# A mixture-of-experts layer on one core: slot tables in two transfers and one expert ahead, and the spare rows' turn and second product in other places

## The reference

```python
for l in range(DEPTH):                      # DEPTH = 1, SEQ = D_MODEL = 1024
    proj = x @ w_in[l]
...
    mix = jnp.concatenate([y_conv, y_sb, y_gla], axis=-1) @ w_out[l]
    x = layer_norm(ALPHA * x + mix, ln1_g[l], ln1_b[l])
    ffn = grouped_moe(x, router_w, router_bias, w1[l], w3[l], w2[l])
    x = layer_norm(ALPHA * x + ffn, ln2_g[l], ln2_b[l])
...
# grouped_moe, 16 experts, D_EXPERT = 512, two experts for each token
for e in range(N_EXPERTS):
    h = jax.nn.silu(t @ w1[e]) * (t @ w3[e])
    y = y + gate[:, e:e + 1] * (h @ w2[e])
```

## Time and profile before

| | us |
|---|---|
| median of 3 runs | 976.55 |
| lowest, highest | 976.47, 983.02 |
| the profiled execution | 981.02 |
| its span, first to last instruction | 979.3 |
| PE busy | 913.9 |
| DVE, ACT, POOL busy | 631.5, 482.2, 284.0 |
| mean granted clock of PE, share of full | 0.973 |

### The profile page before, as it was taken

One profiled execution on the slowest core, in us unless ns is written; L12 is line 12 of the kernel. 1 busy time (PEld: TensorE's weight loads), 2 busy tenths in 40 slices (PEclk: granted clock), 3 DMA queues, 4 the chain that ended last, 5 costly groups with the idle time before them and its releaser, 6 DMA issues.

```text
span 979.3 us, 17611 instructions
## 1 busy us (share of the span) xinstructions
PE 913.9 (93%) x6611; PEld 707.4 (72%) x6611; DVE 631.5 (64%) x831; ACT 482.2 (49%) x755; POOL 284.0 (29%) x292
## 2 busy tenths in 40 slices
PE   8999999999999999979999898999999999998970
PEld 6778998996777777768887475776777767775750
DVE  4211833665564755676556886878787878777885
ACT  3212532225564654561224424666666666665683
POOL 3000000000000000050000486666666666666443
PEclk9999999999999999999999799999999999999995
DMA  9301121001100031059432289999999989999973
GB/s 259 69 22 44 44 58 30 1 2 44 44 22 23 25 73 44 1 182 394 143 129 86 82 245 270 310 334 337 310 324 318 325 299 329 336 330 274 333 261 145
DMA packets 103438, 168.90 MB, mean 172 GB/s; under 512 B 26300, under 2 KB 49980, under 8 KB 103376
## 3 DMA queue, kind: packets, MB, share of 16 engines
q1 hardware_dynamic: 88720, 143.74, 43.2%
q0 software_dynamic: 11616, 23.14, 9.6%
q10 hardware_dynamic: 3040, 1.19, 0.5%
HBM read 143.81 MB, written 24.54 MB: 172 GB/s over the span
## 4 chain that ended last, share of the span: by engine, by line
PE 56%; POOL 16%; DMA 10%; issue 8%; DVE 6%; ACT 3%; POOLq 0%; SPq 0%; DVEq 0%; ACTq 0%
PE bank L887 11%; PE bank L889 11%; PE bank L888 11%; DMA tab<-slot_tokens 9%; PE pz L1003 3%; PE bank L1081 2%; POOL xg L759 2%; POOL tabQ L746 2%; PE pz L887 2%; PE pz L889 2%; PE pz L888 2%; PE bank L1097 2%; POOL sum_scratch L774 2%; POOL sum_scratch L779 2%; POOL slot_tokens L685 2%
## 5 line engine op out<-in xcount | busy, mean ns | idle before, releaser
L1975 DVE TENSOR_TENSOR el<-er,eh 128x1024 fp32r<-128x1024 f32 x192 | 223.6, 1218 | 18.2 <-ACT eh L1568 18.2
L1568 ACT ACTIVATE eh<-er 128x1024 fp32r<-128x1024 f32 x192 | 189.8, 1050 | 7.7 <-PE pz L889 7.7
L632 POOL MEMSET rw<- 128x128 f32 x1 | 0.2, 206 | 415.5 <-DVE mix L1899 415.5
L1906 DVE TENSOR_TENSOR_SCAN Qs<-Qs,own 128x128 f32<-128x128 f32 (+7 forms) x48 | 65.0, 1355 | 69.7 <-ACT Qs L1455 69.7
L887 PE MATMUL pz<-eh,xh 128*128 128x512 f32 x256 | 104.4, 408 | 4.4 <-DVE el L1975 4.4
L887 PE MATMUL bank<-xT_hi,w_hi 128*128 128x512 f32 (+1 forms) x264 | 106.1, 402 | 1.9 <-DVE xT_lo L1791 1.9
L889 PE MATMUL bank<-xT_hi,w_lo 128*128 128x512 f32 (+1 forms) x264 | 102.4, 388 | 0.0
L888 PE MATMUL bank<-xT_lo,w_hi 128*128 128x512 f32 (+1 forms) x264 | 101.8, 386 | 0.0
L888 PE MATMUL pz<-el,xh 128*128 128x512 f32 x256 | 100.8, 394 | 0.0
L889 PE MATMUL pz<-eh,xl 128*128 128x512 f32 x256 | 100.8, 394 | 0.0
L887 PE MATMUL bank<-w_hi,xT_hi 128*128 128x384 f32 x192 | 65.0, 338 | 1.3 <-ACT kteN L1470 1.3
(11 more groups left out here) (337 smaller groups left out, 1873.7 us busy)
## 6 DMA issues: line engine op xcount, KB each, us to landing
er<-in_w_dram SPq DMA_DIRECT2D x192, 512.0 KB, 7.3
w_raw<-in_w_in_dram SPq DMA_DIRECT2D x21, 512.0 KB, 3.9
x_row<-in_x_dram SPq DMA_DIRECT2D x8, 512.0 KB, 9.0
xres<-in_x_dram SPq DMA_DIRECT2D x8, 512.0 KB, 5.6
sum_scratch<-x SPq DMA_DIRECT2D x8, 512.0 KB, 3.9
x_scratch<-x1p SPq DMA_DIRECT2D x8, 512.0 KB, 2.6
cx<-sum_scratch SPq DMA_DIRECT2D x8, 512.0 KB, 8.1
out_dram<-cx SPq DMA_DIRECT2D x5, 512.0 KB, 3.0
```

The lines of the kernel that those rows point to most:

```text
L1568: act.activation(eh[:, p, :], er[:, p, :], ACT.Copy).then_inc(S["eh_ok"], 1)
L1906: dve.tensor_tensor_scan(Qs[:, h, 0:W][:, ::-1], Qs[:, h, 0:W][:, ::-1], own1[:, T - W:][:, ::-1], 0.0, ALU.mult, ALU.max).then_inc(S["sca ...
L1975: dve.tensor_tensor(el[:, p, :], er[:, p, :], eh[:, p, :].bitcast(F32), ALU.subtract).then_inc(S["el_ok"], 1)
```

## The change

**Tables.** The slots of an expert are read with stride: slot 5s + c is row s of block c. A table is then two transfers, one for the whole slots and one that gives each partition the 10 numbers of its five slots, four times over. `load_table` of expert b + 1 stands behind the gathers of b, and `gates` of b - 2 behind that.

**First experts.** For experts 0 to 2 the token numbers of the whole slots come from one product over all 128 slots; for experts 1 and 2 a further small product with `selm` (`spread_slots`, fed by `slot_masks`) spreads them over the quarters. Expert 0's whole rows are gathered as 128 rows of 4 KB by one transfer from `sum_scratch` and transposed by PE (`first_transposes`) into two PSUM banks, in the middle of `spare_gu(0)`; ACT and DVE split them from there in two halves. Eight filling products are dropped. The gather of expert 2 stands between the two `scatter` calls. Counters are shifted to suit (`xTl_ok`, `xTh_ok`, `xg_in`, `idx_in`).

**Places.** `spare_turn(b + 1)` stands behind `hTl` in every expert, and `spare_y` stands whole ahead of the transposes of `hA` (not in the last expert, which is left as it was).

```diff
                 pool.wait_ge(S["first_ok"], 2 * b + 2)
-                for c in range(NB - 1):
+                if b == 0:
+                    pool.indirect_dma_start(xgAs[0][:, :], None, sum_dram, bass.IndirectOffsetOnAxis(firstA[:, 0:1], 0)).then_inc(S["xg_in"], 16)
+                for c in range(NB - 1) if b else ():
                     pool.indirect_dma_start(xg[b % 2][:, c, :], None, x1_quarters, bass.IndirectOffsetOnAxis(firstQ[:, b, c:c + 1], 0))\
                         .then_inc(S["xg_in"], 16)
 
             first_gather(0)
             pool.wait_ge(S["xgB_in"], 16)
-            pool.wait_ge(S["xg_in"], 16 * (NB - 1))
+            pool.wait_ge(S["xg_in"], 16)
             first_gather(1)
             scatter(0)
-            scatter(1)
             pool.wait_ge(S["xBt_ok"], 1)
             pool.wait_ge(S["xTt_ok"], 1)
             pool.wait_ge(S["xgB_in"], 32)
-            pool.wait_ge(S["xg_in"], 32 * (NB - 1))
+            pool.wait_ge(S["xg_in"], 16 * NB)
             first_gather(2)
+            scatter(1)
...
-                for g in range(NQ):
-                    pool.dma_start(tab[r][g * TR:(g + 1) * TR, 2:].rearrange("s (c o) -> s c o", c=NB),
-                                   idl_dram[bass.ds(b * TW, TW), :].rearrange("(c s) o -> s c o", c=NB)).then_inc(S["idx_in"], 16)
+                rows = idl_dram[bass.ds(b * TW, TW), :].rearrange("(s c) o -> c s o", c=NB)
+                blocks = idl_dram[bass.ds(b * TW, TW), :].rearrange("(s c) o -> s (c o)", c=NB)
+                pool.dma_start(tab[r][:, 0:2], rows[0:NQ]).then_inc(S["idx_in"], 16)
+                pool.dma_start(tab[r][:, 2:], blocks.unsqueeze(0).to_broadcast([NQ, TR, 2 * NB])).then_inc(S["idx_in"], 16)
...
-            def step(r, b):
-                load_table(r, b)
-                gates((r + 2) % 4, b - 2)
+            def step(r, b, ahead=True):
                 quarters(r, b)
                 gather(r, b)
+                if ahead:
+                    load_table((r + 1) % 4, b + 1)
+                gates((r + 2) % 4, b - 2)
                 add_rows((r + 2) % 4, b - 2)
 
             def pool_pass(j):
...
                     quarters(3, 3)
                     gather(3, 3)
+                    load_table(0, 4)
                     add_first(1)
                     for u in range(4):
-                        load_table(u, 4 + u)
+                        quarters(u, 4 + u)
+                        gather(u, 4 + u)
+                        load_table((u + 1) % 4, 5 + u)
                         if u:
                             gates((u + 2) % 4, 2 + u)
-                        quarters(u, 4 + u)
-                        gather(u, 4 + u)
-                        if u:
                             add_rows((u + 2) % 4, 2 + u)
...
-                with pool.Fori(2 if isinstance(j, int) else 1, NE // 4) as i:
+                    load_table(0, b0 + 4)
+                with pool.Fori(2 if isinstance(j, int) else 1, NE // 4 - 1) as i:
                     for u in range(4):
                         step(u, b0 + 4 * i + u)
+                for u in range(4):
+                    step(u, b0 + NE - 4 + u, u < 3)
                 for e in (NE - 2, NE - 1):
...
             def slot_tokens(b):
 
-                for part, blocks in enumerate(((NB - 1,), range(NB - 1))):
-                    pe.wait_ge(S["oneh_ok"], 2 * b + part + 1)
-                    for c in blocks:
-                        for i in range(NT):
-                            for g in range(NQ):
-                                last = pe.matmul(sids_bank[b % 2][1 - part][g * TR:(g + 1) * TR, 2 * c:2 * c + 2],
-                                                 oneh[:, b % 2, i, c * TR:(c + 1) * TR], idb[:, :, i],
-                                                 start=(i == 0), stop=(i == NT - 1), skip_group_check=True)
-                    last.then_inc(S["sids_ps"], 1)
+                n = 3 * b - 1 if b else 0
+                pe.wait_ge(S["oneh_ok"], n + 1)
+                for i in range(NT):
+                    for g in range(NQ):
+                        last = pe.matmul(sids_bank[b % 2][1][g * TR:(g + 1) * TR, 0:2], oneh[:, b % 2, i, P:TW], idb[:, :, i],
+                                         start=(i == 0), stop=(i == NT - 1), skip_group_check=True)
+                last.then_inc(S["sids_ps"], 1)
+                pe.wait_ge(S["oneh_ok"], n + 2)
+                for i in range(NT):
+                    last = pe.matmul(sids_bank[b % 2][0][:, 0:2], oneh[:, b % 2, i, 0:P], idb[:, :, i], start=(i == 0), stop=(i == NT - 1),
+                                     skip_group_check=True)
+                last.then_inc(S["sids_ps"], 1)
+
+            def spread_slots(b):
+
+                pe.wait_ge(S["oneh_ok"], 3 * b + 2)
+                pe.matmul(sids_bank[b % 2][0][:, 2:2 + 2 * NQ], selm[:, :], spm[:, b, :, :].rearrange("p g o -> p (g o)"), start=True, stop=True,
+                          skip_group_check=True).then_inc(S["sids_ps"], 1)
 
...
-            spin(4, po[:, 0:GLA_W])
             slot_tokens(1)
             slot_gates(1)
-            spin(4, po[:, 0:GLA_W])
-
-            def spare_gu(b):
-
-                pe.wait_ge(S["xBt_ok"], b + 1)
-                for q in range(NF):
+
+            def first_transposes():
+
+                pe.wait_ge(S["xg_in"], 16)
+                for k in range(NK):
+                    last = pe.transpose(xb[k // 4][:, k % 4, :], xgAs[0][:, k * P:(k + 1) * P], ident[:, :])
+                last.then_inc(S["xTt_ok"], 1)
+
+            def spare_gu(b, qs=range(NF)):
+
+                if qs[0] == 0:
+                    pe.wait_ge(S["xBt_ok"], b + 1)
+                for q in qs:
...
             def pe_block(b, nxt, buf=0, nbuf=0):
-                spare_gu(b)
-                pe.wait_ge(S["xTl_ok"], b + 1)
+                if first_block(b):
+                    spare_gu(b, range(0, 2))
+                    pe.wait_ge(S["selm_ok"], 3 * NQ + 2)
+                    spread_slots(1)
+                    first_transposes()
+                    spare_gu(b, range(2, NF))
+                else:
+                    spare_gu(b)
+                pe.wait_ge(S["xTl_ok"], b + 2)
...
+                if first_block(b):
+                    spread_slots(2)
+
+                spare_y(b)
                 pe.wait_ge(S["hA_ok"], b + 1)
                 for f in range(NF):
                     last = pe.transpose(gA[:, f * P:(f + 1) * P], hA[:, f * P:(f + 1) * P], ident[:, :])
                 last.then_inc(S["hTA_ps"], 1)
-                spare_y(b, range(2, NF))
 
...
-                act.activation(xh[:, :, :], xT[:, :, :], ACT.Copy).then_inc(S["xTh_ok"], 1)
+                if first_block(b):
+                    for r in range(2):
+                        act.activation(xh[:, 4 * r:4 * r + 4, :], xb[r], ACT.Copy).then_inc(S["xTh_ok"], 1)
+                else:
+                    act.activation(xh[:, :, :], xT[:, :, :], ACT.Copy).then_inc(S["xTh_ok"], 1)
...
+            def spare_rows(b):
+
+                bank = sids_bank[b % 2][1]
+                dve.wait_ge(S["sids_ps"], 3 * b if b else 1)
+                link(dve.tensor_scalar(sids[:, b, NB - 1:NB], bank[:, 0:1], quad[:, 0:1], None, ALU.add))
+                dve.tensor_tensor(firstQ[:, b, NB - 1:NB], bank[:, 1:2], sids[:, b, NB - 1:NB], ALU.add).then_inc(S["first_ok"], 1)
+
+            def whole_rows():
+
+                bank = sids_bank[0][0]
+                dve.wait_ge(S["sids_ps"], 2)
+                link(dve.tensor_scalar(sids[:, 0, 0:1], bank[:, 0:1], 1.0 / NQ, None, ALU.mult))
+                dve.scalar_tensor_tensor(firstA[:, 0:1], bank[:, 1:2], 1.0 / NQ, sids[:, 0, 0:1], ALU.mult, ALU.add).then_inc(S["first_ok"], 1)
+
+            def slot_masks(b):
+
+                dve.wait_ge(S["sids_ps"], 3 * b + 1)
+                dve.tensor_tensor(spm[:, b, :, :], maskq[:, :, 0:2], sids_bank[b % 2][0][:, 0:2].unsqueeze(1).to_broadcast([P, NQ, 2]), ALU.mult)\
+                    .then_inc(S["oneh_ok"], 1)
+
+            def quarter_rows(b):
+
+                bank = sids_bank[b % 2][0][:, 2:2 + 2 * NQ]
+                dve.wait_ge(S["sids_ps"], 3 * b + 2)
+                link(dve.tensor_scalar(sids[:, b, 0:NQ], bank[:, 0::2], quad[:, 0:1], None, ALU.add))
+                dve.tensor_tensor(firstQ[:, b, 0:NQ], bank[:, 1::2], sids[:, b, 0:NQ], ALU.add).then_inc(S["first_ok"], 1)
 
...
-                if nxt and not first_block(b):
-                    spare_turn(b + 1, nbuf)
                 piece_lo(b, 6)
                 piece_lo(b, 7)
                 if first_block(b):
-                    slot_rows(2, 0)
-                    slot_rows(2, 1)
+                    spare_rows(2)
+                    slot_masks(2)
                     for c in range(3):
...
                 if first_block(b):
+                    quarter_rows(2)
                     piece_lo(b, NPIECE - 2)
-                    spare_turn(b + 1, nbuf)
                 if nxt:
```

(1 more changed line is left out.)

45 lines of the change are left out of this document (23 added, 22 removed).

## The result

The changed kernel takes 1007.98 us (median of 4 runs, 1006.07 to 1011.37); beside it the kernel before takes 976.51 (4 runs, 973.48 to 983.02). The ratio is 1.032, interval 1.026 to 1.038: slower by 3.2%, against a forecast of 1012.6. The profiled execution took 1008.08, span 1006.4.

The account below looks back on a forecast made before the run. PE was taken as the bound, DVE close behind. Terms +42.4 - 3.3 - 4.85 + 2 x 0.9 = +36.0 us, put on the median 976.55, gave 1012.6 us, ratio 1.037, range 998 to 1034.

Parts of the forecast that it names:

- The loop through the gates: Experts 4 to 14: chain hA, spare turn, gathers, tables, gates copy, yB, back to hA sets a period of 27.65 us.
- the low end: POOL's five gathers per expert, all issued quickly: 6.5 us in place of 6.95, giving 1008 in place of 1012.6.
- the ring: The gates chain over DVE, POOL and ACT in experts 4 to 14: 27.65 us a period, above PE's 23.1.
- The sum over experts 4 to 14: Eleven periods of 27.65 us, 304.2 in place of 261.8: +42.4 us.
- Expert 2: Period of expert 2 on PE: +0.9 us from the whole second product.
- Expert 1: Period of expert 1 on PE: 24.0 in place of 28.85 us, -4.85, as the spare turn leaves DVE's middle.
- the price of the whole product: Spare rows' second product ahead of h's transposes: next product 0.9 us later, +0.9 each in experts 1, 2 and 3.
- the cause given: Expert 1: the turn waited for expert 2's gather behind 16 scatters; eight of these now come after it.
- Expert 0: First expert's new tables, gather and transposes: gain between 0 and 8 us, taken as 3.3.
- The tail: After expert 15's start: nothing moved but the POOL copy of gates 14, so 0.
- The clock: Rival for experts 4 to 14: PE's stops also lower its clock, +15 to +24 us, 1028 to 1037; chance 0.09.
- Rival 1: Gates come in time in experts 4 to 14: only waits removed, 972.4 us, or 959.8 with 0.9 covered; chance 0.09.

Follow-up runs that it names:

- e1: Changed kernel with the copy of the gates ahead of the gathers again; 985.09 us, ratio 0.989.
- e2: Kernel before with only the copy of the gates moved behind the gathers; 1020.51 us, ratio 1.022.
- e6: Changed kernel with the gates copy behind all five gathers but ahead of the two tables; 992.86 us in a single execution.
- e7: Changed kernel with the gates copy behind the third of the five gathers; 975.97 us, ratio 0.998.
- e9: e5 with expert 3's table issued ahead of expert 0's additions; 962.14 us, ratio 0.984.
- e3: As e1, with the spare rows' second product again in two parts around the transposes of hA; 975.99 us.
- e5: As e3, with both scatter calls ahead of the third first gather; 966.49 us, ratio 0.988.
- b1: The kernel before, unchanged, run again for its profile; 980.23 us in a single run.
- e4: Kernel before with the spare rows' second product whole ahead of the transposes of hA; 1002.15 us, ratio 1.005.

## Why the prediction was right, point by point

**The loop through the gates** was right in every link, and e1, e2, e6 and e7 show it as the cause. Its size was 27.65 and came out at 26.93. Link by link, from the timeline above: `hA` to the first gather 4.14 (3.57 predicted; the turn ended 3.30 after `hA`, where I had 3.36, but POOL starts 0.84 us after that end, where I took 0.21 from PE); five gathers 6.26 (6.95); two tables 1.44 (1.18); the copy and ACT's notice 0.28 (0.89); `yB` to `el` 1.46 (1.46); `el` to `hA` 13.35 (13.60). The gathers are the largest miss, and it went past the low end that I had named (6.5): the first is issued beside subtractions on DVE and takes 1.23 us, the other four while DVE stands still, 0.95 to 0.97 each. Where DVE works beside them (e9, periods of 23.09), the four behind the first take 1.63 on average from 653 to 908:

```profile
L763 POOL DMA_INDIRECT xg<-x_scratch,tabQ x43 | 70.1, 1631 | 13.1 <-issue 13.1
```

By the rule of the Trainium skill in "GPSIMD Engine Reference", section "8. Key points", that GpSimd contends with VectorE instructions of two SBUF inputs, this was to be so, and the traces agree: 0.94 to 0.98 us where DVE is idle (after), up to 1.95 beside its subtractions (e9). That the prediction's 1008 for this case is also the measured time is luck: it holds neither the +6.1 of expert 2 nor the -2.4 at the end.

PE stops 1.5 us before the second piece of each expert, where I had said 2 to 3: the ring is shorter, and the stop with it.

**The sum over experts 4 to 14** was mis-sized at +42.4, +32.9 measured: 10 x 0.72 for the period, and 2.2 since expert 14 lasts 25.4 (no table is issued in the last step). That 1012.6 came out so close to 1008 is in part luck, in two ways. The term below has the other sign and takes back 6.1. And the forecast was put on the median of the runs before, while the profiled execution before was 4.5 slower than that median: between the two profiled executions the forecast said +36.0 and the measurement +27.1, 8.9 apart and not 4.6.

**Expert 2** is the step that failed: "in experts 1, 2 and 3 it is +0.9 each". It took +7.0. I had seen that the scatters' second half "ends when all did before, so the later gathers don't come sooner by it", and did not draw the consequence: if experts 0 and 1 end sooner and the first table's gather does not, expert 2 waits for it. Expert 2 starts at 604.97 instead of 616.20, 11 us sooner, but the first table goes out at 602.36, where the kernel before has it at 602.07, and PE stops for 3.28 us and runs at a granted 0.50 behind it. So 6.2 us of the gain of experts 0 and 1 were given back one expert later. e9 shows that an earlier table removes it.

**Expert 1** (-4.9 for -4.85) and expert 3 (+0.9) were right, and so was the price of the whole product, 0.82 for 0.9 in e1 against e3. For the cause given, the gather of expert 2 between the scatters, speaks e5: with all 16 scatters ahead of it again the turn behind it waits 4.08 us and expert 1 takes 25.48. **Expert 0** with its start gave 4.8 instead of 3.3, within its bounds. **The tail** gave 2.4 that I had put at 0: it is 52.7 to 53.0 in every version of the changed kernel and 55.0 to 55.1 in b1, e2 and e4, so it belongs to the change and to none of the parts undone here. It stands behind the last engine row of the timeline: POOL's last issue, of a part of the output, starts 45.72 us after expert 15 in both kernels (969.88 and 999.43), and the span ends 9.4 us after it before and 7.0 after. What ends there, no row shows.

**Rivals.** The clock did not fall in the loop, though PE stops there for 1.5 us and twice for 1 us in each period; a window of one whole turn after:

```profile
704.77:731.70 26.93, 23.55 (x181) 16.63 (x177) 18.50 (x21) 14.78 (x19) 12.31 (x11) 1.00 0.88 284
```

PE is busy for 23.55 of 26.93 us at a granted 1.00, the level of 2.4 GHz. In expert 2 a stop of 3.28 us was followed by a stretch at 0.50, the level of 1.2 GHz. The Trainium skill, "TensorE: Matmul & The Clock Gate", section "Why this matters for your kernels", warns of idle gaps of PE between bursts of products only from some length on, and the short stops of the ring beside the long one of expert 2 agree with that; the two stops of 2.1 us, with a fall in e9 and none in e5, show that the length of a stop alone does not tell it in these runs. Rival 1, gates in time, is what e3 is: 253.96 for experts 4 to 14, where I had written 254.1.

## What to carry to other kernels

In an engine's queue that is served in order, look at what each small instruction is wanted for and by when, before it is put behind something that waits: a copy of 0.25 us behind a gather that waits for a buffer closed a ring over four engines and set the period of the whole loop. Such a ring is read in the waits as long waits of equal count and nearly equal length on several engines; add its links up, compare with the bound engine's own period, and only the excess costs time. And when an early part of a program becomes faster, look for the next chain that did not move with it: a part of the gain can end there.
